# A hybrid attention and mixture-of-experts step: routing on two engines, overflow work behind the first hidden product, last sums on TensorE

## The chip, the cores and the metric

The kernel runs on one core of a Trainium2 chip. A core has TensorE (PE: matrix products; weight loads are shown apart as PEld), VectorE (DVE), ScalarE (ACT), GpSimd (POOL), SyncE (SP, which issues most transfers) and 16 DMA engines, tied together by semaphores that the program sets and waits for. The metric is the device time in microseconds: 516.03 us before, the median of 3 runs (514.69 to 517.61). Less is better.

## The reference

One step of a one-layer streaming encoder on 512 prompt frames and 64 sample frames of width 1024: a normed input projection, sliding-window attention and an HGRN2 recurrence side by side, one output projection, and a mixture of experts. Cut to the part that the change touches:

```python
def hier_moe(h, w_rg, b_rg, w_re, b_re, w_gate, w_up, w_down):
    g_logits = h @ w_rg + b_rg                    # 4 groups; top 1
    p_group = max(softmax(g_logits))
    e_logits = (h @ w_re + b_re)[of that group]   # 4 experts in it; top 2
    e_w = softmax(top2(e_logits)) * p_group       # gates of a token
    out = 0
    for e in range(16):                           # D 1024, expert width 256
        y = (silu(h @ w_gate[e]) * (h @ w_up[e])) @ w_down[e]
        out = out + gates[..., e:e + 1] * y
    return out

x = x + concat(attention, recurrence) @ w_o
x = x + hier_moe(rmsnorm(x, norm2_g), ...)
y = rmsnorm(x, final_norm_g)
```

## The kernel before

The 576 tokens are tiles t = 0 to 4; tile 4 has 64 rows (the sample frames), the others 128. Everything is written out engine by engine (`@block.tensor`, `@block.vector` and so on); an engine works through its list in order, and a `wait_ge` in it holds back all that stands behind. No scheduler moves anything, so the order of the code is the order of the work.

Up to about 287 us of the span the kernel projects, attends and runs the recurrence, tile by tile. The change touches nothing there. Then three stages follow.

*Routing.* For each tile the second norm gives `h2`; TensorE turns it (`turn_h2`), the two halves of the turned tile are copied to `h2T`, and `route` multiplies it with the router's weights. The first three tiles share these two copies between ScalarE (`h2T_act`) and VectorE (`h2T_dve`); for tiles 3 and 4 ScalarE makes both (L967). VectorE adds the bias (`take_logits`), ranks the groups and experts (`pick`), and TensorE counts with small products (L2042, L2046, L2053, L2080, L2081) at which place of which expert each token stands. The slots of tiles 0 and 1 (`slots_of`, L2053) are multiplied behind `route` of tile 4, and the totals (L2080, L2081) ahead of the slots of tiles 2 to 4. The result is `table_tok` (L1537): for each of 16 blocks of up to 128 tokens, one per expert, which rows of `h2_rows` in memory it takes. GpSimd gathers them (`gather`, L735) into `xg`. Ahead of the first gather it issues two transfers of the last norm's gains (L728). Of tile 4, VectorE writes `h2` unscaled and scales it later in `scale_rows` (L1364), behind `pick` of tile 3.

*Blocks of tokens.* `group_of_blocks(i)` handles four blocks (slots 0 to 3), once written out (`first`) and then in a loop of three turns with this input. A block: TensorE turns the gathered rows (L2089); ScalarE rounds them to `xT_hi` (L1010) and VectorE makes the rest `xT_lo` (`x_low`, L1630); the gate and up weights are split the same way (L1016, `gu_low` L1636, four pieces a block); TensorE makes 24 products (L2138 to L2140), ScalarE applies silu (L1072), VectorE multiplies to `hh` (L1672), TensorE turns that (L2150) and multiplies with the down weights (`down`: L2110 to L2112 from split parts in slots 0 and 1, `down_low` L1700; L2118 in full fp32 in slots 2 and 3). GpSimd scatters `y` to `y_pairs` in memory, two rows a token. SyncE loads each expert's 3 MB when its buffer is free. Into the first group VectorE also fits small chains that depend on the routing: `rank_v`, the exponents' arguments (L1543 to L1553) ahead of everything, `over_blocks` (L1572 to L1578) between `gu_low` and `x_low` of block 0, `over_pairs` (L1581 to L1593) ahead of the first `hh`, `weights` (the gates, L1558 to L1562) in slot 0, `over_marks` (L1596 to L1601) at the end of slot 1, `steering` in slot 3. They find what goes beyond 128 tokens of one expert. Before the first block TensorE runs 30 products that only keep it busy (L2123).

*The last stage.* When both scatters of the last blocks have landed, SyncE brings each tile's two rows per token back with two transfers (L610, ten in all). `weigh(t)` (L1715) adds them to `x` on VectorE, one weighted term at a time; ScalarE sums the squares (L1092), GpSimd makes the reciprocal root (L640, L641), `final(t)` (L1722) scales, and SyncE stores. TensorE has nothing to do there. The order on VectorE is `weigh(0)`, `weigh(1)`, then `weigh(t)` and `final(t - 2)` in turn:

```python
for i in range(2):
    dve.wait_ge(pair_in[i][t], 16)
    dve.scalar_tensor_tensor(x[0:r, t, :], pair[0:r, t, i * D:(i + 1) * D], gates[0:r, i, t:t + 1],
                             x[0:r, t, :], ALU.mult, ALU.add).then_inc(sum_ready, 1)
```

## Time and profile before

| what | us |
|---|---|
| median of 3 runs | 516.03 |
| the profiled execution, its own time | 516.82 |
| its span | 515.1 |
| TensorE busy | 463.5 (90% of the span) |
| VectorE busy | 351.7 (68%) |
| ScalarE busy | 249.4 (48%) |
| GpSimd busy | 103.5 (20%) |

The durations below are from the profiled execution; 1.7 us of its time lie outside the span. By engine, the chain that ended last is TensorE for 74% of the span, VectorE for 14%, and ScalarE and the transfers for 4% each. TensorE is busy nearly throughout, with two exceptions in the page's 40 slices: around 285 to 330 us, and from 481 us on, where it does nothing at all.

### The profile page before, as it was taken

The page shows a single profiled execution, that of the slowest core. Times are in us where ns is not written, and L with a number is a line of the kernel's source. Part 1 is how long each engine was busy: PE and PEld are TensorE (multiplying, and loading weights), DVE is VectorE, ACT ScalarE, POOL GpSimd, SP SyncE. Part 2 cuts the span into 40 slices and gives each one's busy share as a digit, 9 for nine tenths or more (in the row PEclk, how much of TensorE's full clock was granted, in tenths as well). Part 3 has the DMA queues.
Part 4 walks back from the last instruction along what each step waited for, and adds up shares of the span by engine and source line. Part 5 has one row for each costly group of instructions (what it writes and reads, how often), then busy time and mean ns, then how long its engine had stood idle before and what let it go on. Part 6 is the DMA issues. An engine that isn't in the chain of part 4 may idle for free.

```text
span 515.1 us, 7205 instructions
## 1 busy us (share of the span) xinstructions
PE 463.5 (90%) x2525; PEld 374.5 (73%) x2525; DVE 351.7 (68%) x674; ACT 249.4 (48%) x472; POOL 103.5 (20%) x167
## 2 busy tenths in 40 slices
PE   6999899999999999999999988899999999999300
PEld 5879799878897777777887777786786787787100
DVE  4877515585676455775664669999798698695176
ACT  6663721553265536343231254686487577573021
POOL 5248001010100000001010032111232223223143
PEclk9999999999999999999999969999999999999855
DMA  8804404004006510610101598999899999810394
GB/s 304 198 11 165 172 0 163 1 1 164 1 2 185 156 56 0 181 46 0 42 15 49 183 331 330 422 416 393 350 350 410 358 357 391 342 65 25 103 325 171
DMA packets 32958, 93.17 MB, mean 181 GB/s; under 512 B 10104, under 2 KB 13312, under 8 KB 26784
## 3 DMA queue, kind: packets, MB, share of 16 engines
q1 hardware_dynamic: 27728, 82.81, 44.9%
q0 software_dynamic: 5200, 9.97, 5.2%
q8 instruction: 17, 0.28, 0.2%
q14 instruction: 13, 0.11, 0.1%
HBM read 87.85 MB, written 13.89 MB: 198 GB/s over the span
## 4 chain that ended last, share of the span: by engine, by line
PE 74%; DVE 14%; ACT 4%; DMA 4%; issue 1%; SPq 1%; POOL 0%; POOLq 0%; ACTq 0%; DVEq 0%
PE ps L1784 8%; PE ps L1786 7%; PE ps L1785 7%; PE ps L2118 5%; PE ps L2138 5%; PE ps L2140 5%; PE ps L2139 5%; PE ps L1996 3%; PE ps L1998 3%; PE ps L1997 3%; DVE gu_lo L1636 3%; DMA pair<-y_pairs 2%; PE ps L2021 2%; PE ps L1939 1%; PE ps L1936 1%; PE ps L2089 1%
## 5 line engine op out<-in xcount | busy, mean ns | idle before, releaser
L1636 DVE TENSOR_TENSOR gu_lo<-we_gu,gu_hi 128x1024 fp32r<-128x1024 f32 x64 | 74.7, 1218 | 0.7
L1016 ACT ACTIVATE gu_hi<-we_gu 128x1024 fp32r<-128x1024 f32 x64 | 63.2, 1055 | 0.0
L2138 PE MATMUL ps<-gu_hi,xT_hi 128*128 128x512 f32 x128 | 52.1, 407 | 3.2 <-DVE xT_lo L1630 3.1
L2140 PE MATMUL ps<-gu_hi,xT_lo 128*128 128x512 f32 x128 | 50.2, 392 | 0.0
L1784 PE MATMUL ps<-hT_hi,w_hi 128*128 128x288 f32 x160 | 48.5, 303 | 1.7 <-DVE w_lo_q L1129 0.8
L2139 PE MATMUL ps<-gu_lo,xT_hi 128*128 128x512 f32 x128 | 50.0, 390 | 0.0
L1784 PE MATMUL ps<-w_hi,hT_hi 128*128 128x512 f32 x96 | 38.9, 405 | 0.5 <-DVE w_lo L1132 0.5
L1785 PE MATMUL ps<-w_lo,hT_hi 128*128 128x512 f32 x96 | 37.5, 390 | 0.0
L1784 PEld LDWEIGHTS ps<-hT_hi,w_hi 128*128 128x128 f32 x160 | 30.0, 188 | 5.0 <-issue 2.6
L2138 PEld LDWEIGHTS ps<-gu_hi,xT_hi 128*128 128x128 f32 x128 | 24.1, 188 | 9.4 <-issue 2.5
L826 ACT ACTIVATE w_hi<-ring,g_col 128x512 fp32r<-128x512 f32 (+1 forms) x48 | 28.7, 680 | 0.0
L1786 PE MATMUL ps<-hT_hi,w_lo 128*128 128x288 f32 x96 | 28.3, 294 | 0.0
L2118 PE MATMUL ps<-we_d,hhT 128*128 128x512 f32 x64 | 28.1, 592 | 0.0
L2140 PEld LDWEIGHTS ps<-gu_hi,xT_lo 128*128 128x128 f32 x128 | 24.0, 188 | 5.2
L2139 PEld LDWEIGHTS ps<-gu_lo,xT_hi 128*128 128x128 f32 x128 | 24.1, 188 | 5.1 <-issue 0.5
L1072 ACT ACTIVATE sg<-ps 128x256 f32<-128x256 f32 x16 | 6.2, 385 | 44.4 <-PE ps L2140 44.4
L1997 PE MATMUL ps<-w_lo,mix_hi 128*128 128x512 f32 x64 | 25.6, 399 | 0.0
L1132 DVE SCALAR_TENSOR_TENSOR w_lo<-ring,g_col,w_hi 128x512 fp32r<-128x512 f32 (+1 forms) x40 | 25.4, 702 | 0.0
L709 POOL COPY qbd<-qa 64x256 f32<-64x256 f32 x18 | 8.0, 446 | 80.6 <-PE ps L1830 44.6
L640 POOL TENSOR_SCALAR ms<-osq 128x4 f32<-128x4 f32 (+1 forms) x5 | 1.0, 195 | 115.5 <-ACT logf L928 115.5
L1630 DVE TENSOR_TENSOR xT_lo<-ps,xT_hi 128x512 fp32r<-128x512 f32 x34 | 21.9, 684 | 2.5 <-ACT xT_hi L1010 2.5
L1785 PE MATMUL ps<-hT_lo_a,w_hi 128*128 128x288 f32 x80 | 23.6, 295 | 0.0
(404 smaller groups left out, 1187.6 us busy)
## 6 DMA issues: line engine op xcount, KB each, us to landing
we_gu<-in_w_gate SPq DMA_DIRECT2D x16, 1024.0 KB, 8.4
we_gu<-in_w_up SPq DMA_DIRECT2D x16, 1024.0 KB, 13.9
we_d<-in_w_down SPq DMA_DIRECT2D x16, 1024.0 KB, 13.7
ring<-in_w_in SPq DMA_DIRECT2D x4, 2048.0 KB, 7.8
pair<-y_pairs SPq DMA_DIRECT2D x8, 512.0 KB, 7.8
ring<-in_w_in SPq DMA_DIRECT2D x3, 1024.0 KB, 8.0
x_first<-in_x_p SPq DMA_DIRECT2D x4, 512.0 KB, 9.6
x<-in_x_p SPq DMA_DIRECT2D x4, 512.0 KB, 3.8
```

Source lines behind the costliest of these rows:

```text
L826: act.activation(w_split(k, w_high(k, c)), w_raw(k, c), ACT.Copy, scale=gain).then_inc(w_hi_done, 1)
L1016: act.activation(gu_hi[slot % 2][:, :, 2 * q:2 * q + 2, :], we_gu[slot][:, :, 2 * q:2 * q + 2, :], ACT.Copy).then_inc(gu_hi_done, 1)
L1132: ins = dve.scalar_tensor_tensor(out, w_raw(k, c), g1_col[:, c:c + 1], hi, ALU.mult, ALU.subtract)
L1636: dve.tensor_tensor(gu_lo[slot][:, :, 2 * q:2 * q + 2, :], we_gu[slot][:, :, 2 * q:2 * q + 2, :], gu_hi[slot % 2][:, :, 2 * q:2 * q + 2, : ...
L1784: pe.matmul(out, stationary[0], moving[0], start=c == 0, stop=False)
L1785: pe.matmul(out, stationary[0], moving[1], start=False, stop=False)
L1786: last = pe.matmul(out, stationary[1], moving[0], start=False, stop=c == KC - 1)
L1997: pe.matmul(out, mix_hi[:, c, 0:r], w_l, start=False, stop=False)
L2118: last = pe.matmul(bank(4 + 2 * (slot % 2) + half), hhT[:, slot % 2, f, :], we_d[slot][:, f, 512 * half:512 * half + 512], start=f == 0, s ...
L2138: pe.matmul(bank(0), xT_hi[:, c, :], gu_h[:, :, c, :], start=c == 0, stop=False)
L2139: pe.matmul(bank(0), xT_hi[:, c, :], gu_l[:, :, c, :], start=False, stop=False)
L2140: last = pe.matmul(bank(0), xT_lo[:, c, :], gu_h[:, :, c, :], start=False, stop=c == KC - 1)
```

## The change

Six edits, all in the three stages told above.

1. `h2T` of tiles 3 and 4 is copied half by ScalarE, half by VectorE, as for the other tiles. VectorE's half of tile 3 stands between the two additions of the second half of `x` of tile 4. `scale_rows` is gone: ScalarE scales tile 4's `h2`, behind its copies. GpSimd clears `xg` before it makes the reciprocal root of tile 4, not after.
2. On TensorE `slots_of(0)` and `slots_of(1)` stand ahead of `route` of tile 4, and the totals behind the last slots. `mark_slots` of tile 4 waits for one signal less. The products that keep TensorE busy are 20, not 30.
3. On VectorE the routing chain (`rank_v` to `route_diff`) stands behind `x_low` of block 0, `over_blocks` behind `weights` in slot 0, `over_pairs` behind `down_low` of slot 1, and the last piece of `gu_low` of block 1 behind the first `hh`. ScalarE's exponentials stand behind its work for block 1.
4. GpSimd issues the transfers of the last gains behind the first two gathers.
5. Each tile's two rows per token come back in one transfer (five of up to 1 MB, not ten).
6. For tiles 1 to 4 TensorE makes `x` plus the second weighted row in PSUM: products of `x` with the unit matrix (`bring_x`; those of tile 4 are made four times, the fourth counts), then of the pair's second half with a diagonal matrix of gates (`diag`, made by VectorE with the weights). VectorE then needs one operation a tile (`weigh_first`), and the order of sums and `final` is new.

The diff, cut to its core:

```diff
             gu_low(0, 0, 0, KC // 2)
-            over_blocks()
             x_low(0, 0)
             x_low(0, 1)
-            gu_low(1, 1, 0, KC // 2)
-            over_pairs()
+            dve.wait_ge(rank_ready, NT + 1)
...
+            dve.tensor_tensor(rb[:, :, 4:5], tops[:, :, 1:2], tops[:, :, 0:1], ALU.subtract).then_inc(route_diff, 1)
+            gu_low(1, 1, 0, 3)
             dve.sem_inc(y_dve, 2)
...
                     x_low(s + 1, 1)
+                    if i is first and slot == 0:
+                        gu_low(1, 1, 3, KC // 2)
...
                         (weights if slot == 0 else steering)()
+                        if slot == 0:
+                            over_blocks()
...
                     if i is first and slot == 1:
+                        over_pairs()
                         over_marks()
```

```diff
@@ def weights
+                dve.wait_ge(gates_ready, 1)
+                for t in range(1, NT):
+                    dve.tensor_scalar(diag[:, t - 1, :], ident[:, :], gates[:, 1, t:t + 1], None,
+                                      ALU.mult).then_inc(diag_ready, 1)
@@ vector, routing
                 if t == NT - 1:
                     chain(last)
+                    if half:
+                        h2T_half(NT - 2)
                     dve.wait_ge(half_copied, len(halved) + half + 1)
@@ tensor, routing
             turn_h2(NT - 1)
-            route(NT - 1)
             for t in range(NT - 3):
                 slots_of(t)
+            route(NT - 1)
...
-            for _ in range(30):
+            for _ in range(20):
                 pe.matmul(ps[:, 3, 0:2 * P], decay_m[:, 0, :], decay_m[:, :, :], start=True, stop=True)
@@ sync, last stage
             for t in range(NT):
-                for i in range(2):
-                    cols = slice(i * D, (i + 1) * D)
-                    sp.dma_start(pair[0:rows_of(t), t, cols], pairs[tok(t), cols]).then_inc(pair_in[i][t], 16)
+                sp.dma_start(pair[0:rows_of(t), t, :], pairs[tok(t), :]).then_inc(pair_in[t], 16)
@@ vector, last stage
+            def weigh_first(t):
+                r = rows_of(t)
+                dve.wait_ge(added, t)
+                dve.wait_ge(pair_in[t], 16)
+                dve.scalar_tensor_tensor(x[0:r, t, :], pair[0:r, t, 0:D], gates[0:r, 0, t:t + 1],
+                                         ps[0:r, 2 * t - 2:2 * t, :].rearrange("p b n -> p (b n)"),
+                                         ALU.mult, ALU.add).then_inc(sum_ready, 1)
@@ tensor, last stage
+            pe.wait_ge(diag_ready, NT - 1)
+            pe.wait_ge(xT_dve, 2 * UNROLL * turns + 2)
+            pe.wait_ge(y_act, UNROLL * turns + 2)
+            pe.wait_ge(y_dve, UNROLL * turns + 2)
+            def bring_x(t, alone):
+                r = rows_of(t)
+                for half in range(2):
+                    pe.matmul(ps[0:r, 2 * t - 2 + half, :], ident[0:r, 0:r], x[0:r, t, 512 * half:512 * half + 512],
+                              start=True, stop=alone)
+            for t in range(1, NT - 1):
+                bring_x(t, False)
+            for _ in range(3):
+                bring_x(NT - 1, True)
+            bring_x(NT - 1, False)
+            for t in range(1, NT):
+                r = rows_of(t)
+                pe.wait_ge(pair_in[t], 16)
+                for half in range(2):
+                    last = pe.matmul(ps[0:r, 2 * t - 2 + half, :], diag[0:r, t - 1, 0:r],
+                                     pair[0:r, t, D + 512 * half:D + 512 * half + 512], start=False, stop=True)
+                last.then_inc(added, 1)
```

How the lists of two engines stand at the places that the prediction speaks of. VectorE, from the last of the routing chain to the start of `over_pairs`, before (`gu_lo` is the weights' low part, `xT_lo` the tokens', `per_expert` belongs to `over_blocks`, `per_pair` and the last `compared` to `over_pairs`):

```order
L1553 TENSOR_TENSOR rb<-rt 128x5
L1636 TENSOR_TENSOR gu_lo_144<-we_gu_148,gu_hi_130 128x2x512 x4
L1572 TENSOR_TENSOR compared<-rank_v,limits 128x16x4
L1574 TENSOR_REDUCE per_expert<-compared 128x16
L1575 TENSOR_TENSOR compared<-upto,per_expert 128x256
L1577 TENSOR_REDUCE per_expert<-compared 128x16
L1578 TENSOR_TENSOR per_expert<-per_expert 128x16
L1630 TENSOR_TENSOR xT_lo<-ps,xT_hi 128x512 x2
L1636 TENSOR_TENSOR gu_lo_145<-we_gu_149,gu_hi_158 128x2x512 x4
L1581 TENSOR_TENSOR compared<-picks,rank_v 128x160
L1583 TENSOR_REDUCE per_pair<-compared 128x10
L1584 TENSOR_TENSOR compared<-picks,per_expert 128x160
```

The same place now, from the table to the first `hh` (`rb` ends the routing chain):

```order
L1536 TENSOR_SCALAR table<-ps 128x16
L1624 TENSOR_TENSOR gu_lo_145<-we_gu_149,gu_hi_131 128x2x512 x4
L1618 TENSOR_TENSOR xT_lo<-ps,xT_hi 128x512 x2
L1632 COPY rank_v<-ps 128x64
L1633 COPY rank_v<-ps 128x32
L1636 TENSOR_REDUCE rt<-logits 128x5
L1637 TENSOR_TENSOR rb<-logits,rt 128x5x4
L1639 TENSOR_TENSOR compared<-picks,logits 128x160
L1641 TENSOR_REDUCE rt<-compared 128x10
L1642 TENSOR_TENSOR rb<-rt 128x5
L1624 TENSOR_TENSOR gu_lo_146<-we_gu_150,gu_hi_159 128x2x512 x3
L1670 TENSOR_TENSOR hh<-sg,ps 128x256
```

The small chains that filled the place between the table and `x_low` stand behind it now or later, and `x_low` follows `gu_low` of block 0 at once. Of the overflow work nothing is left ahead of the first `hh`.

VectorE in the last stage, before:

```order
L1715 SCALAR_TENSOR_TENSOR x<-pair,gates,x 128x1024 x6
L1722 SCALAR_TENSOR_TENSOR pair<-x,stats,g_bc 128x1024
L1715 SCALAR_TENSOR_TENSOR x<-pair,gates,x 128x1024 x2
L1722 SCALAR_TENSOR_TENSOR pair<-x,stats,g_bc 128x1024
L1715 SCALAR_TENSOR_TENSOR x<-pair,gates,x 64x1024 x2
L1722 SCALAR_TENSOR_TENSOR pair<-x,stats,g_bc 128x1024 x2
L1722 SCALAR_TENSOR_TENSOR pair<-x,stats,g_bc 64x1024
```

And now (`ps` is the sum that TensorE made):

```order
L1719 SCALAR_TENSOR_TENSOR x<-pair,gates,x 128x1024 x2
L1728 SCALAR_TENSOR_TENSOR x<-pair,gates,ps 128x1024
L1735 SCALAR_TENSOR_TENSOR pair<-x,stats,g_bc 128x1024
L1728 SCALAR_TENSOR_TENSOR x<-pair,gates,ps 128x1024 x2
L1735 SCALAR_TENSOR_TENSOR pair<-x,stats,g_bc 128x1024
L1728 SCALAR_TENSOR_TENSOR x<-pair,gates,ps 64x1024
L1735 SCALAR_TENSOR_TENSOR pair<-x,stats,g_bc 128x1024 x2
L1735 SCALAR_TENSOR_TENSOR pair<-x,stats,g_bc 64x1024
```

Ten weighted sums became six, and the first `final` stands behind the third of them; one `final` stands between the sums of tiles 3 and 4.

TensorE at the end, now (before, its list ended with the products of the last down weights):

```order
L2132 MATMUL ps<-we_d_156,hhT 128x512 x4
L2174 REGISTER_ALU
L2174 COMPARE_AND_BRANCH
L2178 ISA
L2179 ISA
L2184 MATMUL ps<-x,ident 128x512 x6
L2184 MATMUL ps<-x,ident 64x512 x8
L2196 MATMUL ps<-pair,diag 128x512 x6
L2196 MATMUL ps<-pair,diag 64x512 x2
L97 UNCONDITIONAL_BRANCH
```

Fourteen products with the unit matrix and eight with the gates are new.

## Rows read from the trace of the kernel before

**Rows 1.** stretch: us; busy PE, PEld, DVE, ACT, POOL; clock; DMA share; GB/s

```profile
330.00:350.00 20.00, 19.90 (x98) 16.43 (x97) 19.59 (x25) 13.89 (x19) 3.89 (x4) 1.00 1.02 417
```

**Rows 2.** chain of waits, routing of the last two tiles: start us, us, what

```profile
300.69 0.50 ACT pt L967
```

**Rows 3.** VectorE timeline, routing to fourth block: start us, us, what [idle before]

```profile
307.01 0.18 DVE L1431 TENSOR_TENSOR rt<-picks,ps 64x32 f32<-64x32 f32 x1 [0.71 <-PE ps L2081]
308.55 0.17 DVE L1537 TENSOR_SCALAR table_tok<-ps 128x16 int32<-128x16 f32 x1 [0.69 <-PE ps L2053]
...
308.73 0.21 DVE L1543 COPY rank_v<-ps 128x64 f32<-128x64 f32 x1
...
310.04 4.62 DVE L1636 TENSOR_TENSOR gu_lo<-we_gu,gu_hi 128x1024 fp32r<-128x1024 f32 x4
314.58 0.22 DVE L1572 TENSOR_TENSOR compared<-rank_v,limits 128x64 f32<-128x64 f32 x1
...
316.21 1.29 DVE L1630 TENSOR_TENSOR xT_lo<-ps,xT_hi 128x512 fp32r<-128x512 f32 x2
...
321.95 0.32 DVE L1581 TENSOR_TENSOR compared<-picks,rank_v 128x160 f32<-128x160 f32 x1
...
324.56 0.42 DVE L1672 TENSOR_TENSOR hh<-sg,ps 128x256 f32<-128x256 f32 x1 [0.15 <-DVE per_pair L1593]
...
331.84 0.42 DVE L1672 TENSOR_TENSOR hh<-sg,ps 128x256 f32<-128x256 f32 x1
...
343.71 0.41 DVE L1672 TENSOR_TENSOR hh<-sg,ps 128x256 f32<-128x256 f32 x1
```

**Rows 4.** TensorE timeline, products that keep it busy, first to third block

```profile
308.45 5.16 PE L2123 MATMUL ps<-decay_m 128*128 128x256 f32 x30
314.21 1.16 PE L2089 MATMUL ps<-ident,xg 128*128 128x128 f32 x8 [0.61 <-DMA xg<-h_rows,table_tok]
316.95 0.50 PE L2138 MATMUL ps<-gu_hi,xT_hi 128*128 128x512 f32 x1 [1.58 <-DVE xT_lo L1630]
...
322.53 1.04 PE L2089 MATMUL ps<-ident,xg 128*128 128x128 f32 x8
...
335.02 0.48 PE L2138 MATMUL ps<-gu_hi,xT_hi 128*128 128x512 f32 x1
...
344.26 0.43 PE L2150 MATMUL ps<-ident,hh 128*128 128x128 f32 x2
```

**Rows 5.** GpSimd timeline, the first gather

```profile
309.68 1.11 POOL L735 DMA_INDIRECT xg<-h_rows,table_tok  x1 [5.47 <-DVE table L1539]
```

**Rows 6.** ScalarE timeline, first block

```profile
314.96 1.08 ACT L1010 ACTIVATE xT_hi<-ps 128x512 fp32r<-128x512 f32 x2 [4.58 <-PE ps L2089]
...
322.73 0.39 ACT L1072 ACTIVATE sg<-ps 128x256 f32<-128x256 f32 x1 [1.60 <-PE ps L2140]
```

**Rows 7.** groups of VectorE instructions by shape: x count, busy us, mean ns

```profile
L1243 DVE TENSOR_SCALAR s_buf<-s_buf,small 128x128 f32<-128x128 f32 x4 | 0.9, 282 | 0.0
```

**Rows 8.** TensorE timeline, last full-fp32 products

```profile
473.60 7.03 PE L2118 MATMUL ps<-we_d,hhT 128*128 128x512 f32 x16
```

**Rows 9.** VectorE timeline, the last stage

```profile
502.13 1.28 DVE L1715 SCALAR_TENSOR_TENSOR x<-pair,gates,x 128x1024 f32<-128x1024 f32 x1 [0.86 <-DMA pair<-y_pairs]
...
504.65 2.58 DVE L1715 SCALAR_TENSOR_TENSOR x<-pair,gates,x 64x1024 f32<-64x1024 f32 x2
507.27 2.48 DVE L1722 SCALAR_TENSOR_TENSOR pair<-x,stats,g_bc 128x1024 f32<-128x1024 f32 x2
510.45 1.28 DVE L1722 SCALAR_TENSOR_TENSOR pair<-x,stats,g_bc 64x1024 f32<-64x1024 f32 x1 [0.70 <-POOL stats L641]
```

**Rows 10.** single microseconds of the last stage, columns as in rows 1

```profile
485.00:486.00 1.00, 0.00 (x0) 0.00 (x0) 0.00 (x0) 0.00 (x0) 0.00 (x0) 0.75 0.06 25
489.00:490.00 1.00, 0.00 (x0) 0.00 (x0) 0.28 (x1) 0.00 (x0) 0.00 (x0) 0.50 1.06 430
493.00:494.00 1.00, 0.00 (x0) 0.00 (x0) 1.00 (x1) 0.51 (x2) 0.39 (x1) 0.50 1.04 287
```

More of the change, by code:

```diff
@@ L1726, in _ @@
             weigh(0)
-            weigh(1)
+            weigh_first(1)
+            final(0)
+            weigh_first(2)
+            weigh_first(3)
+            final(1)
+            weigh_first(4)
             for t in range(2, NT):
-                weigh(t)
-                final(t - 2)
-            final(NT - 2)
-            final(NT - 1)
+                final(t)
         @block.tensor
@@ L2077, in _ @@
             rank_own(NT - 1)
+            for t in range(NT - 3, NT):
+                slots_of(t)
             last_rows = rows_of(NT - 1)
```

72 lines of the change are left out of this document (33 added, 39 removed).

## The prediction

> **What bounds the kernel now.** Read first the busy time by stretch: from 330 to 350 us VectorE is busy 19.59 of 20 us, TensorE 19.90, with the DMA engines full [rows 1]. The first group of blocks is therefore limited by both engines, and what VectorE gets to do there must be paid for; later groups are TensorE's. Read then the chain of waits through the routing [rows 2]: it changes between TensorE and ScalarE. Read third VectorE's timeline from the table at 308.55 to the third `hh` (`sg` times the up product, L1672) at 343.71 [rows 3]: 35.16 us with no wait over 0.3 us. The work is fixed, so only the moment at which it starts, what is added and new waits can move its end. TensorE's list at the third `hh`: its second `down` ended at 344.26, and the `hh` was ready just then [rows 3, 4]. In the last stage TensorE has nothing to do from 480.63 (473.60 plus 7.03) [rows 8], the DMA engines are full at 287 to 430 GB/s [rows 10], and VectorE follows the landings: it waited 0.86 us for the last pair of tile 3 and started at 502.13, and `final(4)` ended at 510.45 + 1.28 = 511.73 [rows 9].
>
> **The routing (edits 1 and 2): 1.5 us earlier.** ScalarE's second half copy is 0.50 us on the chain, for tile 4 [rows 2] and once more, the same, for tile 3. VectorE makes it beside ScalarE's first half now, its copy taking 0.1 us longer: 0.8 us gained. The 0.6 us by which tile 4's `h2` is written later is hidden behind `route` of tile 3. The scaling that leaves VectorE stood before a wait, so it gives nothing by itself. Behind `route` of tile 4 TensorE no longer has slots and totals ahead of what VectorE waits for: the wait of 0.71 us at 307.01 [rows 3] goes. The table is ready at 308.55 - 1.5 = 307.05. Bounds: 0.7 (only the wait) to 2.3.
>
> **The gather (edit 4): same wait as before.** Gather 0 was issued at 309.68 and its rows turned from 314.21, 4.53 us later [rows 4, 5]. Now issued at 308.2, landed at 312.7. The gains' transfers no longer run beside it, which may take up to 1 us off; they end long before anybody reads them, and the third gather behind them waits for TensorE in any case. The ten products fewer (30 took 5.16 us [rows 4]) keep the turns from being held up; 20 end by 312.5.
>
> **VectorE to the third `hh` (edit 3 and `diag`): 2.3 us later.** `x_low` can start 0.75 us (314.21 to 314.96) plus one ScalarE copy, 0.64 with its signal, behind the gather [rows 4, 6]: 314.1, not 316.21. But `gu_low` of block 0 takes 4.54 (310.04 to 314.58) [rows 3] and starts at 307.2, so VectorE is free at 311.8 and waits 2.3 us, where before it made the routing chain (1.31, from 308.73 to 310.04) and `over_blocks` (1.63, from 314.58 to 316.21) [rows 3]. TensorE starts block 0 0.74 behind `x_low` [rows 3, 4], at 314.85, 2.1 us earlier than now. 24 products end 5.58 later [rows 4], silu and its signals add 0.2 + 0.44 [rows 6]: the first `hh` at 321.05. VectorE comes there at 314.1 + 1.21 (two `x_low`) + 1.31 + 3 x 1.135 = 320.05 and waits 1.0 us, against 0.15 before [rows 3]. `diag` adds four `tensor_scalar` of 128 x 128. Four of that shape take 0.9 us together [rows 7] (the mean of one is 0.28, so they overlap), and I take 0.9 with the added wait; bounds 0.4 and 1.4. All the rest is moved and costs what it cost. Sum: 307.05 + 35.16 + 0.9 + 2.3 + 1.0 - 0.4 (waits of before that are gone) = 346.0, against 343.71: +2.3 us.
>
> The Trainium skill (VectorE: DVE Perf Modes, "The perf-mode tier table") gives fp32 `tensor_scalar` from SBUF twice the rate of `tensor_tensor`. By it `diag` would be about 0.5 us, an estimate from that table's 1227 ns for 2048 elements plus a fixed part, and the sum +1.9; the row above is nearer to this use and decides.
>
> Does TensorE hide it? The second `hh` comes at 331.84 - 1.5 + 0.9 + 2.3 + 1.0 - 0.4 - 2.6 (`over_pairs`, 321.95 to 324.56, now behind it) = 331.5, and block 2 starts 1.2 later at 332.7, 2.3 us before its 335.02 [rows 3, 4]. The second `down` then ends at 342.0, and TensorE waits 4.4 us for the third `hh`. So block 3 starts late by what VectorE is late, and the fourth `hh` hangs on VectorE too. Afterwards TensorE sets the pace and carries the +2.3 us to the end.
>
> **The last stage (edits 5 and 6): 2.6 us earlier.** TensorE starts at 481.4, when the last `y` is copied. A full fp32 product of 512 columns is 0.86 us (16 records, two to a product, in 7.03) [rows 8]. 14 of them with the unit matrix, the repeats of tile 4 (5.2 us) among them, end at 493.5, long before tile 3 lands, and the end hangs on tile 3: hidden. Per tile two more, 1.72 us, then `weigh_first` at 1.28 as the same operation from SBUF; from PSUM I take no more, bounds 1.2 and 1.5. From the landing of tile 3: 1.72 + 1.28 + `final(1)` 1.28 + sum of tile 4 1.28, then 3.22 (507.23, the end of the last sum, to 510.45) and `final(4)` 1.28 [rows 9]: 10.1 us. Before it was 511.73 - 502.13 = 9.6. The three fewer sums are thus paid back by the wait for TensorE; the gain is only what tile 3 lands earlier, less 0.5. By bytes: 4.2 MB up to tile 3. Tile 0 is whole at about 490.2, a microsecond behind the first at full rate [rows 10], and the 3.15 MB behind it take 7.7 us at the 410 to 430 of the best microsecond, 11.0 at the 287 of the worst [rows 10]: 497.9 to 501.2, against 502.1. I take 499.0, nearer to the fast end, because the transfers of weights, whole as these are now, hold 417 over 20 us [rows 1]. Gain 3.1 - 0.5 = 2.6; bounds -0.5 (no earlier landing) and +3.7. Tile 4 must land by 501.5 for this.
>
> **Sum.** +2.3 - 2.6 = -0.3 us. The profiled execution's own time 516.82 becomes 516.5; it stood 0.8 above the median of the runs, which becomes 516.03 - 0.3 = 515.7.
>
> **Rivals.**
> - *VectorE's new waits are shorter and the pairs stream* (faster). The gather lands 1 us earlier without the gains beside it, `diag` costs 0.5, so +1.0; tile 3 lands at 497.9: -3.7. Sum -2.7 to -3.5, time 512.9. For it: the DMA engines were full while the gather ran. Against it: the second gather ran at the same time and still does.
> - *TensorE's clock falls in the new wait* (slower). TensorE stopped at 480.63 and the granted clock left its upper level, 2.4 GHz, for 1.2 between 485 and 486 [rows 8, 10], some 4.9 us later. The wait ahead of the third `hh` is 4.4 us by my sum. If the clock falls, block 3 starts at half rate. The price from a row: the 30 products before the first block took 5.16 us where 30 of 256 columns at 2.4 GHz take 3.3 [rows 4], so 1.8 us lost before the clock was back. Then +2.3 + 1.8 - 2.6 = +1.5; with an average landing (tile 3 at 500.5, gain 1.1) +3.0: 519.0. It decides from a wait of about the length that the clock outlasted before. The Trainium skill (TensorE: Matmul & The Clock Gate, "What's actually happening") says that the throttled state is the default and activity releases it; by this rule the wait costs twice, and the trace's fall at 485 agrees.
> - *The whole transfers land no earlier.* The last tile has 64 rows, and the rate may belong to memory, not to the size. Then the end gains nothing, -0.5 at worst, and the sum is +2.3 to +2.8: 518.6. For it: the best microsecond of the small transfers already reached 430 [rows 10].
> - *The change does not do what it says in the last stage*: TensorE's first products meet a low clock, 14 x 1.72 = 24 us, and every sum waits. It starts 0.8 us after its last product, so I give this 3 in 100; the time would be above 525.
>
> **Chances.** Forecast 515.7 (own range 513.6 to 517.9): 0.50. Faster rival 0.22. Clock 0.14. Landing 0.11. Low clock at the end 0.03. A measurement of this kernel tells about 0.5% (2.6 us) from no change. Faster by more than that: the faster rival and a little of the forecast, 0.25. Slower: two thirds of the three slow cases, and a little of the forecast, 0.20. Within: 0.55. Range 511.8 to 519.2.
>
> **What would show it.** Routing: `table_tok` written about 307. VectorE: idle of some 2.3 us ahead of the first `x_low` and 1 us ahead of the first `hh`; the third `hh` at 346.0; TensorE idle 3 to 5 us ahead of its turn, at clock 1.00 if no rival holds. Last stage: tile 3's sum starting some 20 us behind TensorE's last product of the blocks if tile 3 lands at 499; `weigh_first` waiting for TensorE, not for transfers. The forecast is wrong if VectorE is not late at the third `hh`, or if the pairs land when they did.

## The result: slower, and the profile after

Five runs of the changed kernel gave 521.71 us in the median (519.04 to 522.99), against 516.93 for the kernel before (five runs, 514.69 to 517.61). The ratio is 1.0092, with a 95% interval of 1.0057 to 1.0127: slower by 4.8 us. The forecast was 515.7 us, range 511.8 to 519.2, so the time lies above the range. The profiled execution took 519.04 us (span 516.8), the fastest of the five.

The view of busy time by stretch of the changed kernel, columns as in [rows 1]:

```profile
330.00:350.00 20.00, 15.46 (x61) 11.79 (x60) 19.66 (x32) 10.77 (x15) 3.56 (x2) 0.85 1.02 419
...
342.00:343.00 1.00, 0.00 (x0) 0.00 (x0) 1.00 (x2) 1.00 (x2) 0.00 (x0) 1.00 0.99 406
343.00:344.00 1.00, 0.00 (x0) 0.00 (x0) 1.00 (x2) 0.71 (x1) 0.00 (x0) 0.98 1.09 451
344.00:345.00 1.00, 0.00 (x1) 0.01 (x1) 1.00 (x3) 0.00 (x0) 0.00 (x0) 0.50 0.96 397
346.00:347.00 1.00, 1.00 (x3) 0.76 (x3) 1.00 (x2) 0.00 (x0) 0.00 (x0) 0.50 0.99 406
350.00:351.00 1.00, 1.00 (x4) 0.81 (x3) 1.00 (x2) 0.00 (x0) 0.79 (x1) 0.61 0.84 352
351.00:352.00 1.00, 1.00 (x6) 0.79 (x5) 0.61 (x1) 0.00 (x0) 0.36 (x1) 1.00 0.57 238
```

TensorE was busy 19.90 of these 20 us before [rows 1] and 15.46 after, and the mean granted clock of the stretch (1.00 is full speed) fell from 1.00 to 0.85. VectorE and the DMA engines are as full as they were. From 344 to past 350 the granted clock is 0.50, which is the lower of its two levels, 1.2 GHz.

VectorE's timeline of the changed kernel, from the table to the fourth `hh` (start us, us, what, idle before and who ended it):

```profile
305.53 0.17 DVE L1534 TENSOR_SCALAR table_tok<-ps 128x16 int32<-128x16 f32 x1 [0.70 <-PE ps L2067]
...
305.70 4.62 DVE L1624 TENSOR_TENSOR gu_lo<-we_gu,gu_hi 128x1024 fp32r<-128x1024 f32 x4
312.57 1.29 DVE L1618 TENSOR_TENSOR xT_lo<-ps,xT_hi 128x512 fp32r<-128x512 f32 x2 [2.25 <-ACT xT_hi L1011]
...
319.52 0.42 DVE L1670 TENSOR_TENSOR hh<-sg,ps 128x256 f32<-128x256 f32 x1 [0.94 <-ACT sg L1073]
...
323.75 0.88 DVE L1549 TENSOR_SCALAR diag<-ident,gates 128x128 f32<-128x128 f32 x4
324.54 0.22 DVE L1560 TENSOR_TENSOR compared<-rank_v,limits 128x64 f32<-128x64 f32 x1
...
330.72 0.41 DVE L1670 TENSOR_TENSOR hh<-sg,ps 128x256 f32<-128x256 f32 x1
...
344.53 0.42 DVE L1670 TENSOR_TENSOR hh<-sg,ps 128x256 f32<-128x256 f32 x1
...
354.22 0.42 DVE L1670 TENSOR_TENSOR hh<-sg,ps 128x256 f32<-128x256 f32 x1 [2.61 <-ACT sg L1073]
```

The reader is to see the two new waits, 2.25 and 0.94 us, and `diag`, whose place on the engine is 0.79 (323.75 to 324.54). From the table to the third `hh` are 39.00 us now; before they were 343.71 - 308.55 = 35.16 [rows 3]. That is +3.84, and with the routing 1.5 us shorter it is the +2.3 of the forecast. The next distance was not forecast: from the third `hh` to the fourth are 9.69 us, where they were 7.31. The fourth in VectorE's timeline of before:

```profile
351.02 0.42 DVE L1672 TENSOR_TENSOR hh<-sg,ps 128x256 f32<-128x256 f32 x1 [0.23 <-ACT sg L1072]
```

TensorE's timeline of the changed kernel at the same place:

```profile
340.79 0.40 PE L2126 MATMUL ps<-we_d_hi,hhT_lo 128*128 128x512 f32 x1
345.00 0.70 PE L2164 MATMUL ps<-ident,hh 128*128 128x128 f32 x2 [3.81 <-DVE hh L1670]
345.60 0.80 PE L2152 MATMUL ps<-gu_hi,xT_hi 128*128 128x512 f32 x1
...
350.03 0.63 PE L2153 MATMUL ps<-gu_lo,xT_hi 128*128 128x512 f32 x1
...
351.08 0.39 PE L2153 MATMUL ps<-gu_lo,xT_hi 128*128 128x512 f32 x1
```

TensorE stands idle for 3.81 us, where in [rows 4] it came to the turn just as `hh` was ready. Its last product ahead of the wait ends at 341.19. The microsecond from 343 to 344 has a mean clock of 0.98, so the clock falls at 343.96, 2.8 us later and inside the wait. Half of block 3's 24 products then run at 0.63 us by the record in place of 0.39. The clock was low for 6.8 us in all, 1 us of it in the wait itself, and the fourth `hh` came 2.4 us later for it.

The last stage: first the last copy of `y`, before and after, then the changed kernel's TensorE, VectorE and GpSimd:

```profile
480.67 0.69 DVE L1665 COPY y<-ps 128x512 f32<-128x512 f32 x1 [2.65 <-PE ps L2118]
```

```profile
483.87 0.69 DVE L1663 COPY y<-ps 128x512 f32<-128x512 f32 x1 [2.65 <-PE ps L2132]
```

```profile
484.71 12.40 PE L2184 MATMUL ps<-x,ident 128*128 128x512 f32 x28 [0.87 <-DVE y L1663]
497.04 3.70 PE L2196 MATMUL ps<-pair,diag 128*128 128x512 f32 x8
502.90 3.84 PE L2196 MATMUL ps<-pair,diag 128*128 128x512 f32 x8 [2.17 <-DMA pair<-y_pairs]
```

```profile
493.75 2.61 DVE L1719 SCALAR_TENSOR_TENSOR x<-pair,gates,x 128x1024 f32<-128x1024 f32 x2 [9.18 <-DMA pair<-y_pairs]
499.11 1.28 DVE L1728 SCALAR_TENSOR_TENSOR x<-pair,gates,ps 128x1024 f32<-128x1024 f32 x1 [2.76 <-PE ps L2196]
...
504.93 1.28 DVE L1728 SCALAR_TENSOR_TENSOR x<-pair,gates,ps 128x1024 f32<-128x1024 f32 x1 [2.15 <-PE ps L2196]
...
507.32 1.27 DVE L1728 SCALAR_TENSOR_TENSOR x<-pair,gates,ps 64x1024 f32<-64x1024 f32 x1
...
510.23 1.29 DVE L1735 SCALAR_TENSOR_TENSOR pair<-x,stats,g_bc 128x1024 f32<-128x1024 f32 x1 [0.44 <-POOL stats L642]
512.21 1.28 DVE L1735 SCALAR_TENSOR_TENSOR pair<-x,stats,g_bc 64x1024 f32<-64x1024 f32 x1 [0.70 <-POOL stats L642]
```

```profile
501.94 0.54 POOL L642 TENSOR_TENSOR stats<-ms,neghalf 128x1 f32<-128x1 f32 x1
...
508.75 1.45 POOL L642 TENSOR_TENSOR stats<-ms,neghalf 128x1 f32<-128x1 f32 x1
...
511.64 0.54 POOL L642 TENSOR_TENSOR stats<-ms,neghalf 64x1 f32<-64x1 f32 x1
```

The pair of tile 3 is there at 502.90. The last copy of `y` began at 483.87, so that is 19.0 us behind it; before, with a last `y` at 480.67, it was 502.13 - 480.67 = 21.5 [rows 9]. From the landing to the end of `final(4)` (513.49) are 10.6 us; before, 9.6. From last `y` to end: 29.6 against 31.1, a gain of 1.4 us.

The sum of this trace from the routing on: -1.5 (routing) + 3.84 (VectorE) + 2.4 (clock) - 1.4 (last stage) = +3.3 us. Ahead of the routing the changed kernel's execution was 1.5 us quicker: the trace of before has a low clock from 280.7 to 284.1 there and this one has none, in a part that the change does not touch. So the spans of the profiled pair differ by less, 516.8 - 515.1 = 1.7 us. Outside the span lie 2.2 us now and were 1.8 (means over all runs of the two kernels), and so it is in every kernel here with the sums on TensorE (2.0 to 2.3) against those without (1.8); why stays open. The times of the pair thus differ by 519.04 - 516.82 = 2.2 us, and the medians by 4.8.

### The profile page after: what moved, and what is told of

Read it like the earlier page. It is cut to its first block, busy times and chain, and to the rows that moved or that the text cites. A ratio compares the mean times of both kernels' runs of the same rounds, so it can differ in the third digit from the quotient of the medians.

```text
span 516.8 us, 7268 instructions
## 1 busy us (share of the span) xinstructions
PE 484.3 (94%) x2559; PEld 381.3 (74%) x2559; DVE 347.7 (67%) x675; ACT 249.4 (48%) x471; POOL 101.1 (20%) x167
## 4 chain that ended last, share of the span: by engine, by line
PE 74%; DVE 14%; DMA 5%; ACT 4%; issue 1%; POOL 1%; SPq 0%; POOLq 0%; DVEq 0%
PE ps L1799 7%; PE ps L1801 7%; PE ps L1800 7%; PE ps L2152 5%; PE ps L2132 5%; PE ps L2154 5%; PE ps L2153 5%; PE ps L2011 3%; PE ps L2013 3%; PE ps L2012 3%; DMA pair<-y_pairs 2%; DVE gu_lo L1624 2%; PE ps L2103 2%; PE ps L2035 1%; PE ps L1954 1%; PE ps L1951 1%
## 5 line engine op out<-in xcount | busy, mean ns | idle before, releaser
L825 ACT ACTIVATE w_hi<-ring,g_col 128x512 fp32r<-128x512 f32 (+1 forms) x48 | 28.7, 680 | 0.0
L1800 PE MATMUL ps<-hT_lo_b,w_hi 128*128 128x288 f32 x80 | 23.6, 295 | 0.0
```

The lines of the kernel that those rows point to most:

```text
L825: act.activation(w_split(k, w_high(k, c)), w_raw(k, c), ACT.Copy, scale=gain).then_inc(w_hi_done, 1)
L1800: pe.matmul(out, stationary[0], moving[1], start=False, stop=False)
```

## The experiments

All were timed in five rounds beside the kernel before, whose median was 516.99, 516.55, 516.61 and 516.02 us in the four sets; ratios are to it. "Held" means that the trace has no granted clock under 1.00 at that place.

| kernel | median us | ratio (95%) | table to 4th hh | wait ahead of 3rd hh | clock at 340 to 353 | last y to end |
|---|---|---|---|---|---|---|
| before | 516.93 | 1 | 42.5 | none | held | 31.1 |
| changed | 521.71 | 1.0092 (1.0057 to 1.0127) | 48.7 | 3.8 | 6.8 us low | 29.6 |
| old order | 517.43 | 1.0004 (0.9983 to 1.0026) | 44.1 | none | held | 31.0 |
| wait filled | 517.56 | 1.0012 (0.9995 to 1.0030) | 46.7 | filled | held | 28.2 |
| moved work alone | 521.62 | 1.0085 (1.0057 to 1.0112) | 46.8 | 3.9 | 3.4 us low | 29.9 |
| last stage alone | 515.92 | 0.9990 (0.9969 to 1.0011) | 42.7 | none | held | 28.7 |
| overflow in slot 3 | 521.28 | 1.0085 (1.0052 to 1.0118) | 43.5 | none | held | 31.3 |
| same, 30 products | 517.05 | 1.0008 (0.9986 to 1.0030) | 41.9 | none | held | 29.1 |
| routing alone | 516.33 | 0.9983 (0.9964 to 1.0002) | 43.5 | none | held | 31.2 |
| whole pairs alone | 517.25 | 1.0003 (0.9986 to 1.0020) | 43.2 | none | held | 30.0 |
| old order, 30 products | 516.18 | 0.9996 (0.9982 to 1.0010) | 43.7 | none | held | 28.4 |
| over_pairs alone moved | 517.69 | 1.0027 (1.0007 to 1.0047) | 46.5 | 2.5 | 3.4 us low | 29.1 |
| x of tile 4 once | 515.14 | 0.9976 (0.9957 to 0.9994) | 43.6 | none | held | 28.8 |
| last stage filled | 517.95 | 1.0024 (1.0006 to 1.0042) | 43.9 | none | held | 31.1 |
| changed, 30 products | 520.20 | 1.0082 (1.0050 to 1.0114) | 48.8 | 3.8 | 6.8 us low | 28.7 |
| changed, all filled | 518.97 | 1.0050 (1.0029 to 1.0071) | 46.7 | filled | held | 28.6 |
| best, block 0 filled | 515.79 | 0.9987 (0.9962 to 1.0012) | 43.8 | none | held | 29.0 |

The columns behind the ratio are of one execution each; the medians are of 5 to 12 (of 5 to 35 for the kernel before). One execution can differ from the next by some tenths of a microsecond up to 1 us in such a column: "whole pairs alone" has the same first group as before and 43.2 in place of 42.5, because its gathered rows came later.

**Old order.** VectorE's order of before, all else as changed:

```diff
+            (routing chain)
             gu_low(0, 0, 0, KC // 2)
+            over_blocks()
             x_low(0, 0)
             x_low(0, 1)
-            (routing chain)
-            gu_low(1, 1, 0, 3)
+            gu_low(1, 1, 0, KC // 2)
+            over_pairs()
```

> The changed kernel with VectorE's order of before in the first group (routing chain, then over_blocks ahead of x_low, over_pairs ahead of the first hh, no piece of gu_low held back); all else as changed. Theory A (VectorE comes 2.3 us late to the third hh, TensorE's wait there lets its clock fall, and that costs 2 to 3 us more): the third hh comes about 0.9 us earlier after the routing than in the kernel before, TensorE waits under 0.5 us there, no stretch at half clock between 335 and 360 us, and the time is 514 to 516 us, 5 to 7 below the changed kernel. Theory B (the loss is in the routing or the last stage, VectorE's order is worth little): 519 to 522 us, and the wait ahead of the third hh goes without the time.

517.43 us, 4.3 below the changed kernel: the loss sits in the moved VectorE work. But it is no gain over before either, though the table is 1.5 us earlier, and both expected ranges are missed (514 to 516, and 519 to 522). Its trace shows what took the gain there: the clock is low from 315.1 to 318.5, inside block 0, and again from 499.4 to 502.8, in the last stage, and VectorE waits 0.82 us ahead of `rank_v` (on this wait more below, at "routing alone").

**Wait filled.** On TensorE, ahead of the third `hh`:

```diff
+                    if i is first and slot == 2:
+                        for _ in range(18):
+                            pe.matmul(ps[:, 3, 0:P], ident[:, :], ident[:, :], start=True, stop=True)
                     pe.wait_ge(hh_ready, s + 1)
```

> The changed kernel with 18 small products of the unit matrix with itself on TensorE behind the second down product, in the place where it waits for the third hh; they compute nothing that is used. Theory A: VectorE's third hh stays where it is, the clock stays at 2.4 GHz from 330 to 360 us, the fourth hh comes 2 to 2.5 us earlier than in the changed kernel, and the time is 2 to 3 us below it, 518.5 to 520. Rival A2 (the wait alone costs, the fall of the clock is hidden by VectorE, which is late at the fourth hh too): the clock stays up and the time stays within 0.7 us of the changed kernel.

Its results are thrown away. TensorE's timeline, and one microsecond of the busy time by stretch:

```profile
343.37 4.18 PE L2164 MATMUL ps<-ident 128*128 128x128 f32 x36
347.39 0.45 PE L2167 MATMUL ps<-ident,hh 128*128 128x128 f32 x2
```

```profile
346.00:347.00 1.00, 1.00 (x11) 1.00 (x11) 1.00 (x2) 0.06 (x1) 0.00 (x0) 1.00 1.01 418
```

The third `hh` is as late as in the changed kernel (39.5 us behind the table), yet the clock holds and block 3 runs at full rate: the fourth `hh` comes 7.3 us behind the third, as before. 517.56 us, 4.1 below the changed kernel and more than the 1.7 to 3.2 us expected. VectorE is as late as without the fill, so this shows directly that the clock, and not only VectorE's lateness, is in the loss. How much of it is less sure: the traces differ by 2.4 us behind the third `hh`, the medians by 4.1, and the same fill in a kernel with 30 products gives less (see "changed, all filled").

**Moved work alone.** The mirror image: the kernel before with only the moved VectorE and ScalarE work.

```diff
             gu_low(0, 0, 0, KC // 2)
-            over_blocks()
             x_low(0, 0)
             x_low(0, 1)
-            gu_low(1, 1, 0, KC // 2)
-            over_pairs()
+            (routing chain)
+            gu_low(1, 1, 0, 3)
```

> The kernel before with only VectorE's new order in the first group and ScalarE's exponentials moved behind its work for block 1; no diagonal matrices, routing, gathers and last stage as before. Theory A: VectorE idles 2 to 2.5 us ahead of the first x_low and 1 us ahead of the first hh, the third hh comes 2.5 to 3 us later than in the kernel before (346.5), TensorE waits 4 us or more there, the clock may fall in it, and the time is 3 to 5.5 us above the kernel before: 519.5 to 522. Theory B: within 1 us of the kernel before.

521.62 us: the whole loss from this edit alone. TensorE waits again:

```profile
345.74 0.70 PE L2154 MATMUL ps<-ident,hh 128*128 128x128 f32 x2 [3.90 <-DVE hh L1671]
```

**Last stage alone**, the kernel before with whole pairs, `diag` and the sums on TensorE:

```diff
-                for i in range(2):
-                    sp.dma_start(pair[0:rows_of(t), t, cols], pairs[tok(t), cols]).then_inc(pair_in[i][t], 16)
+                sp.dma_start(pair[0:rows_of(t), t, :], pairs[tok(t), :]).then_inc(pair_in[t], 16)
```

> The kernel before with only the new last stage: whole transfers of pairs, sums of x on TensorE, and the four diagonal matrices made in slot 0. Theory A: from the last y to the last store 1.4 us less than before, the diagonal matrices 0.9 us more on VectorE in the first group, in sum 0 to 1 us below the kernel before: 516 to 517. Theory B (the last stage loses): 518 or more.

515.92 us, 0.5 to 1.1 below before by ratio and by medians, which is inside the interval of no change. Its trace has 28.7 us from the last `y` to the end, 2.3 better than before.

**Overflow in slot 3, with 20 and with 30 products.** VectorE's order of before up to the first `hh`, but `over_pairs`, `over_marks` and `diag` behind `steering`, in slot 3, and then the same with the old count of products ahead of block 0:

```diff
+                        if slot == 3:
+                            over_pairs()
+                            over_marks()
+                            diags()
```

> The changed kernel with VectorE's order of before up to the first hh, but over_pairs (2.6 us), over_marks and the four diag products moved to slot 3, behind steering. Theory A (what counts is only that VectorE reaches the third hh before TensorE would stop): the third hh needs no wait, TensorE's granted clock stays at 1.00 from 340 to 360, the fourth hh isn't late either, and the time is 512 to 515, some 7 to 9 us below the changed kernel. Rival (VectorE's work is only pushed on, it is late at the fourth hh or at the head of the second group): TensorE waits there by the same 2 to 4 us, and the time is 516 or above.

> As the kernel with the overflow work in slot 3, but with 30 products ahead of the first block, as before, and not 20. Theory A (10 products fewer let block 0 begin at the low clock in some executions, 3.4 us at half rate between 315 and 319 as the trace with VectorE's old order showed): no half clock behind 315, and the median 1 to 2 us below the same kernel with 20. Rival (the low clock there comes and goes with the start of the stage, not with the count): the two are within 0.7 us, or the 30 are slower by up to 1 us because the turns of the gathered rows wait for them.

521.28 and 517.05 us: the first misses its theory by 6 us, and ten products make 4.2 us (the intervals of the two ratios do not meet). TensorE's timelines, first with 20 products, then with 30:

```profile
309.68 4.63 PE L2137 MATMUL ps<-decay_m 128*128 128x256 f32 x20
314.41 1.65 PE L2103 MATMUL ps<-ident,xg 128*128 128x128 f32 x8
318.02 0.50 PE L2152 MATMUL ps<-gu_hi,xT_hi 128*128 128x512 f32 x1 [1.95 <-DVE xT_lo L1620]
...
319.94 0.63 PE L2152 MATMUL ps<-gu_hi,xT_hi 128*128 128x512 f32 x1
```

```profile
307.97 5.47 PE L2137 MATMUL ps<-decay_m 128*128 128x256 f32 x30
313.28 1.06 PE L2103 MATMUL ps<-ident,xg 128*128 128x128 f32 x8
316.32 0.50 PE L2152 MATMUL ps<-gu_hi,xT_hi 128*128 128x512 f32 x1 [1.97 <-DVE xT_lo L1620]
```

With 20 they run at the low rate to the end (4.63 us for 20, 5.47 for 30), and after the same wait of 2 us the clock falls again at 319.0, while products are running. The trace with 20 has a further low stretch in the last stage, from 503.3 to 506.7, and 31.3 us from last `y` to end against 29.1. Each execution lists its mean clock, and twice the span times what that lacks to 1 is the time at half rate: 36.7 us in the mean of the six runs with 20, 24.5 with 30. Half of the difference, 6 us, is what it can cost at most; 4.2 were measured. The rival of the slot 3 kernel held too (516 us or above): the fifth `hh` comes 17.15 us behind the fourth, 14.9 in the kernel with the routing alone, so the pushed work is late at the next group.

**Routing alone** (old order and last stage, 30 products) and **whole pairs alone** (the transfer of the diff above, the sums left on VectorE).

> The kernel before with only the routing edits (ScalarE and VectorE sharing the copies, slots_of moved, the gains' transfers behind the gathers) and ScalarE's exponential moved; VectorE's order, 30 products and the last stage are those of before. Theory A: the table is ready 1.5 us earlier (about 307 where the stretch at 280 runs at half clock, 305.5 where not) and the end comes 1 to 1.5 us earlier: 515.3 to 516. Rival: TensorE's low clock at the start of the blocks is fixed to when it began, so the 1.5 us are given back in block 0, and the time is that of before within 0.5 us.

> The kernel before with only the pairs brought by one transfer of 8 KB rows each in place of two; the sums stay on VectorE. Theory A (my forecast: whole transfers land earlier): tile 3 lands 2 to 3 us earlier measured from the last y, and the time is 1 to 2 us below before. Rival (the landing belongs to the bytes and to the 64 rows of the last tile): within 0.5 us of before, or up to 1 us above it because the first sum of tile 0 must now wait for both halves. The rest of what the changed last stage gave would then be due to TensorE's sums.

516.33 us for the routing: the table is 11.92 us behind tile 3's last turn of `h2`, 13.31 before, so the 1.4 us are there in the trace; in the medians only 0.9 us by the ratio remain, and its interval includes 1. The trace shows where part of them goes, in VectorE's timeline between the table and `gu_low`:

```profile
309.81 0.23 DVE L1624 COPY rank_v<-ps 128x64 f32<-128x64 f32 x1 [0.82 <-PE ps L2077]
```

The edits of the routing put the totals behind the last slots, and the routing chain, which in VectorE's old order stands ahead of `gu_low`, now waits 0.82 us for them; before it followed the table at once (308.55 and 308.73 [rows 3]). The third `hh` comes 36.2 us behind the table in place of 35.2. In the changed kernel the chain stands behind `x_low` and does not wait. So the early table and the moved chain belong together, and every kernel here with the new routing and the old order pays this wait.

517.25 us for the whole pairs: no gain that can be measured, against 1 to 2 us expected. Its trace does not test the landing, because with ten sums VectorE sets the end: it starts 9.9 us behind the last `y` (9.1 before), now that it waits for tile 0 whole, and from then on waits for no pair at all. Tile 3 had landed at the latest 19.05 us behind the last `y`, where 21.5 were needed before.

**Old order with 30 products; over_pairs alone moved; x of tile 4 once; last stage filled.** The first undoes two edits; the three others start from it:

```diff
-            for _ in range(20):
+            for _ in range(30):
                 pe.matmul(ps[:, 3, 0:2 * P], decay_m[:, 0, :], decay_m[:, :, :], start=True, stop=True)
```

```diff
             gu_low(1, 1, 0, KC // 2)
-            over_pairs()
...
                     if i is first and slot == 1:
+                        over_pairs()
                         over_marks()
```

```diff
-            for _ in range(3):
-                bring_x(NT - 1, True)
             bring_x(NT - 1, False)
```

```diff
-            bring_x(NT - 1, False)
             for t in range(1, NT):
...
+                if t == NT - 2:
+                    bring_x(NT - 1, True)
+                    bring_x(NT - 1, False)
                 pe.wait_ge(pair_in[t], 16)
```

> The changed kernel without the moved VectorE work and with 30 products ahead of the first block, as before: the routing edits, the whole transfers and the sums on TensorE are all that is left of the change. Theory A (10 products fewer let the clock fall inside block 0, as in both traces with 20 and VectorE's old order, and each such fall costs 1.7 us): no half clock in block 0, table to last y 372 to 373 us against 373.8 with 20, and a time of 514 to 516. Rival (the falls come by chance of when the stage starts): within 0.7 us of the same kernel with 20, 517.

> As the kernel with the old order and 30 products, but over_pairs (2.6 us of VectorE) is moved behind the second hh, as the change has it; the routing chain and over_blocks stay where they were. Theory A (the change loses because VectorE, with all of the work moved, has waits of its own ahead of the first x_low and the first hh): the first hh comes a little earlier, VectorE waits up to 1 us for it, the third hh is late by no more than that, TensorE waits under 1.5 us for it and keeps its clock; the time is within 1 us of the old order. Rival (any work between the second and the third hh is paid in full): third hh 2.6 us later, TensorE waits over 3 us, clock falls, time 2 to 4 us above.

> As the kernel with the old order and 30 products, but x of tile 4 is multiplied once and not four times. Theory A (the repeats only hold TensorE's clock until the pairs land): TensorE stops some 5 us earlier, the granted clock falls before tiles 1 and 2 land, each tile's pair of products takes 3.8 to 4 us in place of 2, and the time is 2 to 4 us above. Rival (VectorE and the transfers set the end, TensorE's products are hidden): within 0.7 us, since the first sum of tile 1 waits for the first tile on VectorE anyway.

> As the kernel with the old order and 30 products, but of the products of x of tile 4 three times two stand where they did and two times two more (3.4 us) behind those of tile 2's pair, where TensorE waits 1.2 to 2.3 us for the pair of tile 3. Theory A (the low clock of 499 to 503 in the traces with the old order begins in that wait): the clock holds to the last product, and the time is 0 to 1.5 us below the one without. Rival (the 3.4 us delay tile 3's products more than a fall of the clock costs): 0.5 to 2 us above.

The old order with 30 products gives 516.18 us, with no low clock in block 0. That is 1.2 below the same with 20, but the two stand in different sets: by the ratios they differ by 0.4 us, and the intervals overlap, so no gain is shown here. (The distances from the table to the last `y` in its expectation are 200 us too large: they are 173.4 us, and 173.8 with 20.)

With `over_pairs` alone moved the time is 517.69, 1.5 us above that, between the two expectations; the third `hh` comes 37.8 us behind the table in place of 36.4. TensorE's timeline and the busy time by stretch:

```profile
342.32 0.40 PE L2123 MATMUL ps<-we_d_hi,hhT_lo 128*128 128x512 f32 x1
345.25 0.65 PE L2161 MATMUL ps<-ident,hh 128*128 128x128 f32 x2 [2.53 <-DVE hh L1671]
```

```profile
344.00:345.00 1.00, 0.00 (x0) 0.00 (x0) 1.00 (x2) 1.00 (x2) 0.00 (x0) 1.00 1.02 422
345.00:346.00 1.00, 0.75 (x3) 0.47 (x3) 1.00 (x3) 0.24 (x1) 0.00 (x0) 0.73 1.07 447
346.00:347.00 1.00, 1.00 (x3) 0.81 (x4) 1.00 (x2) 0.00 (x0) 0.00 (x0) 0.50 0.95 393
```

Here the clock falls behind a wait of 2.53 us: at 345.5, after work has begun again. Behind the waits of 2 us ahead of block 0 it fell in one of the two traces above and not in the other. That the wait is the cause is not shown by one trace, since the clock also falls in busy stretches (in this one at 280.6); what is shown is that it did not hold.

With x of tile 4 multiplied once the time is 515.14, where 2 to 4 us more were expected. TensorE waits 4.14 us for the pairs and its clock does fall:

```profile
481.40 7.25 PE L2181 MATMUL ps<-x,ident 128*128 128x512 f32 x16 [0.88 <-DVE y L1665]
492.79 9.80 PE L2191 MATMUL ps<-pair,diag 128*128 128x512 f32 x16 [4.14 <-DMA pair<-y_pairs]
```

```profile
490.00:491.00 1.00, 0.00 (x0) 0.00 (x0) 0.65 (x1) 0.00 (x0) 0.00 (x0) 1.00 0.98 418
491.00:492.00 1.00, 0.00 (x0) 0.00 (x0) 0.96 (x2) 0.00 (x0) 0.00 (x0) 0.54 1.00 426
494.00:495.00 1.00, 1.00 (x3) 0.48 (x2) 0.00 (x0) 0.14 (x2) 0.68 (x2) 0.50 1.03 434
```

But only tiles 1 and 2 are multiplied at the low clock, and they are there early. From last `y` to the end are 28.8 us, with four times 28.4. So the repeats gain nothing here. Filling the wait ahead of tile 3 with four more products gives 517.95, 1.8 us worse (the intervals of the two ratios just overlap), as its rival had it: the fill was still running when the pair came (products of the fill to 502.97, tile 3's from 502.90 without a wait).

**Changed with 30 products; changed with all waits filled; best with block 0 filled.** The first two are the changed kernel with the edits above (30 products; and then the 18 products in the wait and x once as well). The third is the kernel with x once and, behind the turns of the first gathered rows:

```diff
             turn_half(0, 1, x_turned_b)
+            for _ in range(10):
+                pe.matmul(ps[:, 3, 0:2 * P], decay_m[:, 0, :], decay_m[:, :, :], start=True, stop=True)
```

> The changed kernel with 30 products ahead of the first block in place of 20, nothing else. Theory A (the loss in the median is 1.5 us more than the profiled execution of the changed kernel shows, because in the other executions the clock also falls inside block 0, as in the traces with 20 products and the old order): the ratio to before falls from 1.009 to 1.004 to 1.007, a time of 518.5 to 520.5; the fall ahead of the third hh stays. Rival (block 0 starts early enough in the changed order, so 20 do): the ratio stays at 1.008 to 1.011.

> The changed kernel, its moved VectorE work included, with 30 products ahead of the first block, the 18 products with the unit matrix in the wait ahead of the third hh, and x of tile 4 multiplied once. Theory A (the moved work costs little by itself, what it costs is the clock): no half clock between 316 and 490, ratio to before 0.997 to 1.001. Rival (VectorE's late third hh is paid in full through the groups that follow): ratio 1.002 to 1.005, 1.5 to 3 us above the kernel with the old order and x once.

> The kernel with the old order, 30 products and x of tile 4 once (0.998 of before), with 10 of the same products of 256 columns more in TensorE's wait of some 2 us between the turns of the first gathered rows and the first x_low. Theory A (that wait holds the clock low or lets it fall): the half clock ends before block 0 in the trace, and the time is 1 us below, 0.996 of before. Rival (the low clock behind the routing ends at its own moment, and the wait is short enough): within 0.3% of the same kernel without them.

Ratios 1.0082, 1.0050 and 0.9987. The ten products do not bring the changed kernel down as theory A had it (the ratio was to fall to 1.007 or less), so its missing 1.5 us are not settled; the time at half rate falls from 32.2 us (mean of five runs) to 27.6 (six runs), which points the same way without being enough. With all waits filled 3 us above before by medians remain: the rival, that the moved work costs something of its own. From "changed, 30 products" to this kernel the fill, with x once, gives 1.2 us by the medians and 1.7 by the ratios, where it gave 4.1 with 20 products; the traces agree better, with the fourth `hh` 2.1 us earlier here and 2.0 there. In the trace of the all-filled kernel the fourth `hh` comes 46.7 us behind the table at a clock of 1.00 throughout, 4.2 more than before, less 1.5 from the routing. The fill of block 0 changes nothing that can be measured.

The fastest kernel is the one with VectorE's old order, 30 products, the new routing and last stage, and x of tile 4 once: 515.14 us, 0.2% below before, 6.6 below the changed kernel by the medians and 6.0 by the ratios. Its near twin with block 0 filled has an interval that includes 1, so I would not call it more than level with before.

## Why the prediction was wrong

**The routing, 1.5 us earlier: right.** From the last turn of tile 3's `h2` to the table are 11.8 us after and 13.3 before. What it overlooked is that the totals come later for it, which costs 0.8 us wherever the routing chain keeps its old place.

**The gather: right.** 4.5 us from issue (306.70) to turn (311.19), as in [rows 4, 5].

**VectorE, +2.3 at the third hh: right, term by term.** New waits 2.25 and 0.94 (forecast 2.3 and 1.0), `diag` 0.8 (0.9). TensorE's wait was 3.81 (4.4).

**"So block 3 starts late by what VectorE is late ... Afterwards TensorE sets the pace and carries the +2.3 us to the end": the failed step.** The sum priced TensorE's wait as a delay and nothing more. Shown in its place: the clock falls in the wait, and the fourth `hh` is 4.7 us late net of the routing, not 2.3, and the last `y` with it. The kernel with only the wait filled shows it: its clock holds and it is 4.1 us lower. The rival named the mechanism and gave it 0.14. Its weight came from one row, the 4.9 us that the clock outlasted at 480 to 485 [rows 8, 10]; that is one sample of something that varies. The traces here have falls 2.3 us (changed with 30 products), 2.4 (x once), 2.7 (over_pairs alone moved), 2.8 (changed) and 4.0 us (moved work alone) behind the last product. One long survival says nothing about how short a wait can be harmful. Its price, 1.8 us, was also low: 2.4 in the trace. The Trainium skill (TensorE: Matmul & The Clock Gate, "What's actually happening") has the throttled state as the default and activity as what releases it; the five traces agree, each with 0.50 granted behind the wait and 1.00 again some microseconds into the work.

**The last stage, -2.6: half of it.** The landing of tile 3 was 2.4 us earlier where 3.1 were forecast, and the end came 10.6 us behind it, not 10.1: the sum of tile 3 began 2.03 us behind the landing (1.72 in the forecast), and `final(3)` waited 0.44 us for GpSimd's small operation, which took 1.45 us. Before, that operation was as long, 1.58 us, but hidden behind the longer sums. In this trace -1.4; over all runs the stage alone is worth 0.5 us by the ratio, inside the interval of no change, and whole transfers alone nothing measurable.

**The ten products fewer, costed at nothing: wrong in one of three pairs of kernels.** I asked only whether they delay the turns. With the overflow in slot 3 the ten are worth 4.2 us, and the time at half rate is 12 us shorter with them. In the old order the difference is 0.4 us by the ratios, in the changed order 0.1%, both with intervals that overlap. So they are no shown part of this loss.

**The sum.** +2.3 + 2.4 - 1.4 = +3.3 us in place of -0.3, and with the 0.4 us more outside the span, which the forecast did not have, +3.7, against +4.8 measured. The profiled execution was the fastest of five with a mean clock of 0.975, while the slowest three had 0.964 to 0.967, some 8 to 12 us more at half rate each, which would be 4 to 6 us of time at most. Where those lost it was not seen, since no trace of them exists, and the kernel made to test one place (block 0, with 30 products) did not settle it. Nor is it settled why the wait-filled kernel stands at 1.0012 and the all-filled one at 1.0050.

## What to carry to other kernels

When a change makes TensorE wait for a few microseconds, price the wait twice: once as delay, and once for the products behind it at half rate; here that held from waits of some 2.5 us up, whatever a single row showed the clock to have survived. Moving work off a critical engine's list is free only if that engine does not then stand waiting earlier: VectorE lost 3.2 us in front of work that it had to do anyway. Products that seem to do nothing may hold the clock, and each such group (here 30, 20 and the repeats of x) is to be tested alone, since one was worth 4 us in one kernel and nothing that could be measured in two others. Compare medians first and traces second: one trace with a low stretch more or less can hide or feign a gain of 1 to 2 us.

## What the hardware did that was not expected

- The granted clock can fall behind a short wait, after work has started again: at 319 in the kernel with the overflow in slot 3, 1 us into block 0, and at 345.5 in the one with `over_pairs` alone moved.
- It also falls in stretches in which TensorE counts as busy: 280.7 to 284.1 in the kernel before. Of the 17 traces 13 have one or two such stretches of 3.4 us between 236 and 286 us, where all kernels have the same code, and 4 have none. The mean clock varies from run to run of one program, and with it the time: the changed kernel took 519.04 us at 0.975 and 522.99 at 0.964.
- GpSimd's `tensor_tensor` on one column took 1.45 us beside VectorE's `final(2)` at 508.75 in the changed kernel, and 0.54 while VectorE was idle (511.64). Beside `weigh_first`, one of whose inputs lies in PSUM, it took 0.54 too (501.94). That the kind of VectorE operation decides is not shown: in "changed, all filled" it took 0.54 beside a `final` as well (502.81).
